# Rotary partner rows by DMA instead of a permutation product, a small chain moved to PSUM, and one activation table for Ln and Exp, in a two-layer hybrid decoder kernel

## The chip, the cores and the metric

The kernel runs on one core of one Trainium2 chip, with five engines that work in parallel and wait for one another by semaphores: TensorE (PE, matrix products; PEld is its weight load), VectorE (DVE), ScalarE (ACT), GpSimd (POOL) and SyncE (SP), which here only issues DMAs. The metric is the device time of one execution in microseconds, lower is better; the time before is the median of three runs.

## The reference, cut to what matters

```python
def reference(x, ln1_g, w_in, qk_norm_g, ...):          # x: 1 x 512 x 1024, two layers
    for l in range(DEPTH):
        h = rmsnorm(x, ln1_g[l])
        proj = h @ w_in[l]                               # 1024 -> 3588 columns
        q = partial_rope(rmsnorm(q, qk_norm_g[l, 0]), cos, sin)   # 4 heads x 2 x 64
        k = partial_rope(rmsnorm(k, qk_norm_g[l, 1]), cos, sin)
        o_a = diff_attention(q, k, v, lam, lambda_init, subln_g[l])
        o_b = sc_b * causal_dwconv(sc_c * sc_h, sc_conv_w[l])
        o_c = s5_mixer(...)                              # diagonal complex scan, 16 groups
        o_d = mamba2_mixer(z, xbc, dt_raw, ...)          # dt = softplus(dt_raw + dt_bias)
        x = x + concat(o_a, o_b, o_c, o_d) @ w_out[l]
        h2 = rmsnorm(x, ln2_g[l])
        g = causal_dwconv(h2 @ ffn_w_gate[l], ffn_conv_w[l])
        x = x + (silu(g) * (h2 @ ffn_w_up[l])) @ ffn_w_down[l]

def partial_rope(x, cos, sin):                           # the first 16 of 64 dimensions
    x1, x2 = x[..., :8], x[..., 8:16]
    rot = concatenate([x1 * cos - x2 * sin, x1 * sin + x2 * cos])
    return concatenate([rot, x[..., 16:]])
```

Dimension i of the first 16 is thus mixed with its partner, dimension i + 8 or i - 8, with a sign. Everything is float32.

## The kernel before

Activations lie transposed, channels on the 128 partitions and the 512 tokens along the row. All products with the large weights go by units: a unit is one block of 128 output channels. Each weight unit passes through four engines. SyncE loads it into one of two `raw` buffers (L260), as soon as GpSimd has read the unit before last (`wl_full`). ScalarE rounds it to a high half `wh` (`prep`, L697). GpSimd computes the low half `wl` = raw - wh (`low`, L287). TensorE then makes three passes over the unit: low activations by `wh` (L386), high by `wh` (L388), high by `wl` (L396), eight products of 128x512 each where the input has 1024 channels. There are two buffers of each kind, so a copy for unit g waits until TensorE has left the high half of unit g - 2. VectorE multiplies the finished bank by the norm factor (`scaled`, L942).

Each engine works through one order written out by hand; a late instruction holds up all behind it. In each layer the 28 units of the input projection come first, numbered s = 0 to 27 below:

- Units 0 and 1 are the S5 input; `dt_rows` and `dt_turn` bring the four step-size columns into bank 5. Units 2 to 7 are the Mamba-2 inputs. VectorE scales each into `pad` and applies four taps (`taps_in_bank`, L959 to L962); ScalarE takes the SiLU from the bank (L790). Between them VectorE computes the step sizes, a softplus by a series, on 128x16 tiles `s16` (`m2_dt`, `m2_log`, `m2_series` with L1021, `m2_steps`). In ScalarE's order, the copy of unit s + 2 comes ahead of the SiLU of unit s and behind that of unit s - 1.
- Units 8 to 15: gate, Mamba-2 products, short convolution. GpSimd makes S5 rotation tables (`table`) and the imaginary part of each S5 scan (`s5_imaginary`) between its low halves.
- Units 16 to 23 are q and k of the four heads, called tiles t = 0 to 7 (t = s - 16); VectorE scales tile t into `G[:, t % 2]`, ScalarE squares it, and after unit 17 + t TensorE makes the group mean (`qk_mean`, L531, bank 4) and the permutation product with the gain folded in (L533, bank 5). ScalarE computes the inverse root by Ln (L715) and Exp (L717); VectorE finishes the tile in `qk_finish`: gain by cosine (L1260), partner by sine (L1262), sum (L1263), norm (L1265, `qk_done`). On every second s VectorE also runs an S5 scan (`s5_scan`), on the others its second half (`s5_back`); before the first tile it waits for the norm of the Mamba-2 output (`m2_rms`).
- Units 24 to 27 are v. Then 16 attention steps (4 heads by 4 query blocks): scores, maxima (L1272), Exp (L832), combination (L1279 to L1281), transpose (L563), product with v (L572); once per head Ln (L842) and Exp (L846) of the output norm. Units of the output projection are put beside some steps (`BESIDE`).

The feed-forward part of a layer is 44 units in and 16 units of 11 blocks down. Which activation table is resident isn't written in the kernel; the build places a load ahead of a function that the resident one doesn't have.

Of the kernel before, what the change touches and what calls it, by code (L numbers as in the profile page):

```python
# [14 lines left out]
L = 2  # L15
# [4 lines left out]
ROPE = 16  # L20
THETA = 500000.0
# [24 lines left out]
for _name, _n in [("ident", P), ("ones", P), ("tri", P), ("perm", P), ("block", P), ("cap", P), ("eps", 1)]:  # L46
    CONSTS[_name] = slice(_o, _o + _n)
    _o += _n
# [3 lines left out]
for _name, _n in [("g1", KD), ("g2", KD), ("qkg", 2), ("subg", 1), ("oneml", 1), ("scw", 6),  # L52
                  ("s5d", 2), ("bglu", 2), ("m2w", 24), ("m2b", 6),
                  ("dtb", M2H), ("alog", M2H), ("m2d", 2), ("m2g", 2), ("ffw", 3 * FF), ("wdt", KD * M2H)]:
    PARAMS[_name] = (_o, _n)
    _o += _n
# [10 lines left out]
def build(nc, A):  # L67
    with ExitStack() as ctx:
# [48 lines left out]
        def early(name, shape, dt=F32):  # L117
# [21 lines left out]
        permg = sb("permg", [P, 2, P])  # L139
# [13 lines left out]
        ident, ones, tri, perm, block1, cap = [  # L153
            cst[:, CONSTS[k]] for k in ("ident", "ones", "tri", "perm", "block", "cap")]
# [38 lines left out]

        sqk_ready, qk_rms, qk_done, v_ready = [sem(n) for n in ("sqk_ready", "qk_rms", "qk_done", "v_ready")]
# [56 lines left out]
        def _(sp):  # L251
# [106 lines left out]
        def _(pe):  # L358
# [167 lines left out]
            def qk_mean(t):  # L526
# [39 lines left out]
            def attend(n):  # L566
                h, q = n // NQ, n % NQ
                if q == 0:
# [15 lines left out]
            for l in range(L):  # L584
# [64 lines left out]
                for n in range(STEPS):  # L649
# [13 lines left out]
                    if n:  # L663
                        attend(n - 1)
                    if n > NQ and n % NQ == 2:
                        head_sum(HEAD_BANK[n // NQ - 1])
                attend(STEPS - 1)
# [15 lines left out]
        def _(act):  # L683
# [34 lines left out]

            def rms():
                act.wait_ge(act_bank[7], nth(act_bank[7]))  # L720
# [27 lines left out]
            for l in range(L):  # L748
# [34 lines left out]
                for s in range(1, NIN):  # L783
# [15 lines left out]
                    if s == 9:  # L799
                        m2_head(0)  # L800
# [50 lines left out]
                for n in range(STEPS):  # L851
# [7 lines left out]
                    if n == 0:  # L859
                        for i, gate in enumerate((sA, sB)):  # L860
                            act.wait_ge(act_bank[i], nth(act_bank[i]))
                            fn(gate[:, :], bank[i][:, :], ACT.Sigmoid, bias=par_of(l, "bglu", i)).then_inc(glu_full, 1)
                    if n == 1:
# [49 lines left out]
        def _(dve):  # L913
# [81 lines left out]

            def m2_dt(l):

                a, e = [s16[:, i, :] for i in (0, 1)]
                by_head = [P, NQ, M2H]
                dve.wait_ge(dve_bank[5], nth(dve_bank[5]))  # L1000
                tt(a.rearrange("p (a b) -> p a b", a=NQ), bank[5][:, 0:16].rearrange("p (a b) -> p a b", a=NQ),
                   par_of(l, "dtb", 0, M2H).unsqueeze(1).broadcast_to(by_head), ADD).then_inc(dve_free[5], 1)
                dve.wait_ge(dve_free[5], freed(dve_free[5]))
                stt(e, a, -1.0, a, MUL, ALU.max).then_inc(dt_abs, 1)
                own(ts(a, a, 0.0, None, ALU.max))

            def m2_log():

                e, s, sq, rec = [s16[:, i, :] for i in (1, 2, 9, 11)]
# [3 lines left out]
                after(tt(s, e, rec, MUL))  # L1013
                own(tt(sq, s, s, MUL))
# [558 lines left out]
```

## Time and profile before

| | |
|---|---|
| median of 3 runs | 1472.79 us (1471.87 to 1472.96) |
| the profiled execution | 1473.24 us, span 1471.4 us |
| TensorE busy | 1395.4 us (95%) |
| VectorE, ScalarE, GpSimd busy | 943.8, 569.9, 685.7 us |
| chain that ended last | 84% TensorE, 10% VectorE, 3% ScalarE |
| input projection of layer one, unit 2 to unit 27 | about 48 to 274 us |
| attention of layer one | about 275 to 366 us |

The profile is one execution on the chip. Its rows give the line of the instruction, the engine, output and inputs by name; an idle time in brackets is followed by what ended it. The "chain that ended last" is followed back from the last instruction, at each step to what released it.

### The profile page before, as it was taken

What the parts mean: (1) busy time and instruction counts of PE and PEld (TensorE: products, weight loads), DVE (VectorE), ACT (ScalarE), POOL (GpSimd) and SP (SyncE); (2) the same over time, 40 slices, a digit from 0 to 9 for tenths busy, and PEclk for the clock granted to TensorE, in tenths of its full rate; (3) what the DMA queues carried; (4) which work ended last, traced back from release to release, by engine and by line L of the source; (5) the groups of instructions that cost most, each with busy time, mean ns of one, the idle gap of its engine ahead of it and who ended that gap; (6) DMA issues with size and microseconds to landing.
All of it is one profiled execution on the core that took longest, in us unless ns stands there. A gap on an engine that the chain in (4) does not pass through costs nothing.

```text
span 1471.4 us, 15836 instructions
## 1 busy us (share of the span) xinstructions
PE 1395.4 (95%) x6116; PEld 1074.4 (73%) x6116; DVE 943.8 (64%) x1221; ACT 569.9 (39%) x805; POOL 685.7 (47%) x368
## 2 busy tenths in 40 slices
PE   3989999798999999999999999998899999999999
PEld 1777656476788888888877775665677888888887
DVE  7778887564677713777228788865657774067740
ACT  3342556456532312222333335645664332123221
POOL 1645768312444443444456456862134444444452
PEclk9999989999999999999999998998999999999999
DMA  5221111111332332323232211111123333223332
GB/s 185 71 73 58 44 53 55 36 33 33 107 101 92 111 98 87 95 91 116 85 100 72 61 55 58 52 42 33 40 54 112 99 100 118 83 86 101 104 101 97
DMA packets 33627, 117.41 MB, mean 80 GB/s; under 512 B 3728, under 2 KB 3856, under 8 KB 33552
## 3 DMA queue, kind: packets, MB, share of 16 engines
q1 hardware_dynamic: 33264, 115.35, 24.9%
q8 instruction: 49, 0.80, 0.2%
q10 hardware_dynamic: 288, 1.05, 0.2%
q14 instruction: 26, 0.21, 0.0%
HBM read 114.28 MB, written 2.10 MB: 79 GB/s over the span
## 4 chain that ended last, share of the span: by engine, by line
PE 84%; DVE 10%; ACT 3%; issue 2%; DMA 1%; POOL 1%; SPq 0%; DVEq 0%; POOLq 0%
PE bank L386 25%; PE bank L388 24%; PE bank L396 24%; PE bank L437 2%; DVE s L1021 1%; PE bank L533 1%; PE bank L448 1%; DVE ml L967 1%; PE bank L446 1%; PE bank L415 1%; PE bank L531 1%; DMA raw<-in_w_first 1%; DVE G L1281 1%; PE bank L572 1%; DVE xl L933 1%
## 5 line engine op out<-in xcount | busy, mean ns | idle before, releaser
L287 POOL TENSOR_TENSOR wl<-raw,wh 128x1024 fp32r<-128x1024 f32 (+3 forms) x208 | 501.7, 2413 | 679.5 <-ACT wh L697 458.5
L386 PE MATMUL bank<-xl,wh 128*128 128x512 f32 x1152 | 303.4, 404 | 35.8 <-ACT wh L697 24.9
L386 PEld LDWEIGHTS bank<-xl,wh 128*128 128x128 f32 x1152 | 217.8, 192 | 109.7 <-issue 39.7
L697 ACT ACTIVATE wh<-raw 128x1024 fp32r<-128x1024 f32 (+3 forms) x208 | 218.3, 1050 | 196.9 <-PE bank L388 191.2
L388 PE MATMUL bank<-xh,wh 128*128 128x512 f32 x1152 | 287.9, 392 | 0.0
L396 PE MATMUL bank<-xh,wl 128*128 128x512 f32 x1152 | 286.1, 390 | 0.0
L388 PEld LDWEIGHTS bank<-xh,wh 128*128 128x128 f32 x1152 | 218.5, 190 | 46.1
L396 PEld LDWEIGHTS bank<-xh,wl 128*128 128x128 f32 x1152 | 216.4, 188 | 45.2 <-issue 0.3
L971 DVE TENSOR_TENSOR x<-x,bank 128x512 f32<-128x512 f32 x64 | 44.0, 687 | 219.7 <-PE bank L396 219.7
L386 PE MATMUL bank<-ml,wh 128*128 128x512 f32 x512 | 136.3, 408 | 0.0
L388 PE MATMUL bank<-mh,wh 128*128 128x512 f32 x512 | 128.4, 391 | 0.0
L396 PE MATMUL bank<-mh,wl 128*128 128x512 f32 x512 | 127.5, 389 | 0.0
L386 PEld LDWEIGHTS bank<-ml,wh 128*128 128x128 f32 x512 | 97.8, 194 | 24.5 <-issue 3.0
L388 PEld LDWEIGHTS bank<-mh,wh 128*128 128x128 f32 x512 | 96.9, 189 | 20.9
L396 PEld LDWEIGHTS bank<-mh,wl 128*128 128x128 f32 x512 | 96.1, 188 | 20.0
L1303 DVE TENSOR_TENSOR G<-G 128x512 f32<-128x512 f32 x44 | 105.2, 2391 | 4.6
L893 ACT ACTIVATE G<-G 128x512 f32<-128x512 f32 x44 | 27.8, 632 | 204.4 <-DVE G L954 204.4
L949 DVE TENSOR_SCALAR G<-pad,par_all 128x512 f32<-128x512 f32 x48 | 94.3, 1964 | 1.5
L942 DVE TENSOR_TENSOR G<-bank,rbc 128x512 f32<-128x512 f32 x76 | 52.2, 687 | 63.7 <-PE bank L396 61.4
L942 DVE TENSOR_TENSOR pad<-bank,rbc 128x512 f32<-128x512 f32 x60 | 41.4, 691 | 53.9 <-PE bank L396 43.3
L896 ACT ACTIVATE mh<-G 128x512 fp32r<-128x512 f32 x44 | 27.7, 630 | 111.1 <-DVE G L1303 111.1
L1305 DVE TENSOR_TENSOR ml<-G,mh 128x512 fp32r<-128x512 f32 x44 | 47.3, 1074 | 31.2 <-ACT mh L896 31.2
(264 smaller groups left out, 1529.9 us busy)
## 6 DMA issues: line engine op xcount, KB each, us to landing
raw<-in_w_gu SPq DMA_DIRECT2D x88, 512.0 KB, 3.5
raw<-in_w_in SPq DMA_DIRECT2D x52, 512.0 KB, 3.5
raw<-in_w_dn SPq DMA_DIRECT2D x32, 704.0 KB, 4.1
raw<-in_w_oe SPq DMA_DIRECT2D x16, 384.0 KB, 3.0
raw<-in_w_ol SPq DMA_DIRECT2D x16, 256.0 KB, 2.6
x<-in_x SPq DMA_DIRECT2D x8, 256.0 KB, 6.1
raw<-in_w_first SPq DMA_DIRECT2D x4, 512.0 KB, 6.7
out_x<-x SPq DMA_DIRECT2D x8, 256.0 KB, 4.7
```

The costliest lines, as they stand in the source:

```text
L287: tt(wl[:, p, 0:cols], raw[:, p, 0:cols], wh[:, p, 0:cols].bitcast(F32), ALU.subtract).then_inc(wl_full, 1)
L386: mm(bank[b][:, :], wh[:, p, k * P:(k + 1) * P], lo[:, k, :], start=(k == 0), stop=False)
L388: w = mm(bank[b][:, :], wh[:, p, k * P:(k + 1) * P], hi[:, k, :], start=False, stop=False)
L396: w = mm(bank[b][:, :], wl[:, p, k * P:(k + 1) * P], hi[:, k, :], start=False, stop=(k == K - 1))
L437: mm(bank[2 + c][:, :], bmat[r:r + SH, c, j // 4, :], u[r:r + SH, j // 4, :], start=True, stop=True).then_inc(dve_bank[2 + c], 1)
L697: fn(wh[:, p, 0:cols], raw[:, p, 0:cols], ACT.Copy).then_inc(wh_full, 1)
L893: fn(G[:, 1, :], G[:, 0, :], ACT.Silu).then_inc(g_silu, 1)
L942: tt(out, bank[b][:, :], rbc[:, :], MUL).then_inc(unit_out, 1)
L949: after(ts(out, pad[:, p, 4:4 + T], weights[n - 1], None, MUL))
L971: tt(x[:, o, :], x[:, o, :], bank[p][:, :], ADD).then_inc(resid, 1)
L1303: tt(G[:, 3, :], G[:, 1, :], G[:, 2, :], MUL).then_inc(h_ready, 1)
L1305: tt(ml[:, i, :], G[:, 3, :], mh[:, i, :].bitcast(F32), SUB).then_inc(hid_ready, 1)
```

## The change

1. *Partner rows.* The host permutes the columns of q and k so that the rotated dimensions of both components of a head lie in partitions 48 to 79, with partners in neighbouring rows. SyncE, ahead of the weight load of unit s + 4, waits until VectorE has written q/k unit s, and issues two DMAs of 16 rows each, which copy even rows onto odd ones and back into a `partner` buffer (one is `G[:, 5]`, one is new). `qk_finish` multiplies this buffer by a gain of its own (`partg`) and by the sines, which VectorE has copied once per layer into bank 5, and writes into bank 4. The permutation product, its matrix and its scaled copies go. The mean product now claims bank 4 against `qk_done`. Before the first tile of a layer VectorE clears both buffers.
2. *Step sizes.* Intermediate results of the softplus chain (`raw_dt`, `rec`, `q`) move from `s16` to columns of bank 5; `m2_dt` writes its sum twice, to `s16` and to the bank, and `m2_log` the quotient twice, so the chain has 20 instructions in place of 18.
3. *ScalarE's order.* The SiLU of unit s comes one step later, so the copy of unit s + 3 is now ahead of it. The Exp of the decays goes a step later as well.
4. *Tables.* The set that holds both Ln and Exp is loaded explicitly before the norms, after each gelu and sigmoid, and before the Mamba-2 exponentials.

```diff
@@ SyncE's loop over the weight units
                 if g >= 2:
                     sp.wait_ge(wl_full, g - 1)
+                s = g % (len(UNITS) // L) - 4
+                if 16 <= s < 24:
+                    sp.wait_ge(unit_out, unit_out_of(g // (len(UNITS) // L), s))
+                    for to, of in ((0, 1), (1, 0)):
+                        sp.dma_start(partner[s % 2][ROT0 + to:ROT1:2, :],
+                                     G[ROT0 + of:ROT1:2, s % 2, :]).then_inc(partner_in[s % 2], 16)
                 sp.dma_start(raw[:, g % 2, 0:cols], src[l, i]).then_inc(raw_full[g % 2], 16)
@@ TensorE, qk_mean
-                claim(4, act_free[4])
+                claim(4, qk_done)
                 mm(bank[4][:, :], block1, G[:, 2, :], start=True, stop=True).then_inc(act_bank[4], 1)
-                claim(5, qk_done)
-                mm(bank[5][:, :], permg[:, t % 2, :], G[:, t % 2, :], start=True, stop=True).then_inc(dve_bank[5], 1)
@@ TensorE, attend
+                if n == 0:
+                    pe.wait_ge(qk_done, 8 * (l + 1))
@@ ScalarE
+            def ln_exp_tables():
+                nc.scalar.preload_act_table_set("natural_log_exp_and_others")
             def rms():
+                ln_exp_tables()
                 act.wait_ge(act_bank[7], nth(act_bank[7]))
...
-                    if 2 <= s <= 7:
+                    if 3 <= s <= 8:
                         act.wait_ge(conv_out, nth(conv_out))
-                        fn(xbc[:, s - 2, :], bank[unit_bank(s)][:, :], ACT.Silu).then_inc(xbc_silu, 1)
-                    if s == 6:
+                        fn(xbc[:, s - 3, :], bank[unit_bank(s - 1)][:, :], ACT.Silu).then_inc(xbc_silu, 1)
+                    if s == 7:
                         act.wait_ge(decay_go, nth(decay_go))
...
                     if s == 9:
+                        ln_exp_tables()
                         m2_head(0)
@@ VectorE, parameters
+                ts(par_of(l, "partg"), par_of(l, "partg"), QK ** -0.5, None, MUL)
-                for i in range(2):
-                    ts(permg[:, i, :], perm, par_of(l, "qkg", i), None, MUL)
@@ VectorE, step sizes
+            def small(i):
+                return bank[5][:, 32 + 16 * i:48 + 16 * i]
...
-                e, s, sq, rec = [s16[:, i, :] for i in (1, 2, 9, 11)]
+                e, s, sq, rec = s16[:, 1, :], s16[:, 2, :], s16[:, 9, :], small(1)
                 after(ts(rec, e, 2.0, None, ADD))
                 after(nc.vector.reciprocal(rec, rec))
-                after(tt(s, e, rec, MUL))
-                own(tt(sq, s, s, MUL))
+                tt(s, e, rec, MUL)
+                after(tt(rec, e, rec, MUL))
+                own(tt(sq, rec, s, MUL))
...
-                sq, q = [s16[:, i, :] for i in (9, 10)]
+                sq, q = s16[:, 9, :], small(2)
                 after(ts(q, sq, 1.0 / 17, None, MUL))
                 for c in (15, 13, 11, 9, 7, 5, 3):
                     after(stt(q, q, 1.0 / c, sq, ADD, MUL))
@@ VectorE, qk_finish
-                dve.wait_ge(dve_bank[5], nth(dve_bank[5]))
-                after(tt(bank[5][:, :], bank[5][:, :], sinT, MUL))
-                after(tt(bank[5][:, :], q, bank[5][:, :], ADD))
+                dve.wait_ge(partner_in[p], 32 * (4 * l + t // 2 + 1))
+                dve.wait_ge(act_free[4], nth(act_free[4]))
+                after(stt(bank[4][:, :], partner[p], par_of(l, "partg", p), bank[5][:, :], MUL, MUL))
+                after(tt(bank[4][:, :], q, bank[4][:, :], ADD))
                 dve.wait_ge(qk_rms, nth(qk_rms))
-                tt(q, bank[5][:, :], G[:, 3 + p, :], MUL).then_inc(qk_done, 1)
+                tt(q, bank[4][:, :], G[:, 3 + p, :], MUL).then_inc(qk_done, 1)
@@ VectorE, step s == 15
                         s5_back(l, 1)
+                        nc.vector.memset(partner[0], 0.0)
+                        nc.vector.memset(partner[1], 0.0)
+                        dve.wait_ge(yz_ready, 2 * (l + 1))
+                        own(copy(bank[5][:, :], sinT))
```

## Rows read from the trace of the kernel before

**Rows 1.** The page: busy time of the engines; the chain that ended last.

```profile
PE 1395.4 (95%) x6116; PEld 1074.4 (73%) x6116; DVE 943.8 (64%) x1221; ACT 569.9 (39%) x805; POOL 685.7 (47%) x368
...
PE 84%; DVE 10%; ACT 3%; issue 2%; DMA 1%; POOL 1%; SPq 0%; DVEq 0%; POOLq 0%
```

**Rows 2.** TensorE's waits: line, releaser, us in total, times, longest.

```profile
PE bank L386 <- ACT wh L697: 24.9, 5, 17.5
```

**Rows 3.** Windows: two rotary units; after an attention wait.

```profile
core 0: us, PE busy (x) PEld busy (x) DVE busy (x) ACT busy (x) POOL busy (x), PEclk, DMA share, GB/s
207.93:226.45 18.52, 18.52 (x65) 11.38 (x65) 15.30 (x22) 12.57 (x16) 15.58 (x12) 1.00 0.17 57
...
347.70:352.00 4.30, 4.30 (x11) 2.69 (x10) 1.46 (x3) 4.24 (x7) 0.00 (x0) 0.50 0.02 4
```

**Rows 4.** TensorE's timeline, convolution stage, both layers: start, us, [idle before <- releaser].

```profile
80.61 3.78 PE L386 MATMUL bank<-xl,wh 128*128 128x512 f32 x8 [4.20 <-ACT wh L697]
...
799.05 3.66 PE L386 MATMUL bank<-xl,wh 128*128 128x512 f32 x8 [2.66 <-ACT wh L697]
```

**Rows 5.** Timelines of VectorE, GpSimd and ScalarE, first layer, convolution stage.

```profile
68.02 7.74 DVE L1021 SCALAR_TENSOR_TENSOR s<-s 128x16 f32<-128x16 f32 x7
...
75.80 1.27 POOL L311 TENSOR_TENSOR ex<-ex,s5h 128x512 f32<-128x512 f32 x1
...
79.01 0.60 ACT L790 ACTIVATE xbc<-bank 128x512 f32<-128x512 f32 x1 [11.37 <-DVE bank L962]
```

**Rows 6.** Two lines of VectorE alone: count, then ns as min/median/max.

```profile
L1021 DVE SCALAR_TENSOR_TENSOR s<-s x14: 174/973/2424, 68.0 to 793.2; 128x16 f32<-128x16 f32 x14
...
L961 DVE SCALAR_TENSOR_TENSOR bank<-pad,par_all,bank x24: 754/756/757, 56.9 to 809.2; 128x512 f32<-128x512 f32 x24
```

**Rows 7.** Timelines of TensorE and ScalarE in attention, first layer.

```profile
324.96 0.44 PE L563 MATMUL bank<-cst,G 128*128 128x128 f32 x2 [1.59 <-DVE G L1281]
...
331.98 1.28 ACT L842 ACT_TABLE_LOAD   x1
...
343.06 0.44 PE L563 MATMUL bank<-cst,G 128*128 128x128 f32 x2 [1.61 <-DVE G L1281]
344.59 0.49 PE L572 MATMUL bank<-G,v 128*128 128x128 f32 x2 [1.09 <-DVE ssum L1288]
346.16 0.90 PE L563 MATMUL bank<-cst,G 128*128 128x128 f32 x3 [1.09 <-DVE G L1281]
```

**Rows 8.** The chain that ended last, convolution stage: start, us, what.

```profile
56.46 1.81 PE bank L388 x8
...
84.39 2.58 PE bank L388 x8
```

**Rows 9.** The same chain in the rotary stage of the first layer.

```profile
185.42 2.08 PE bank L533 x2
...
199.57 0.86 PE bank L533 x2
```

**Rows 10.** Timelines of GpSimd and VectorE in the rotary stage, around tile 3.

```profile
206.29 2.39 POOL L287 TENSOR_TENSOR wl<-raw,wh 128x1024 fp32r<-128x1024 f32 x1
...
207.97 0.69 DVE L942 TENSOR_TENSOR G<-bank,rbc 128x512 f32<-128x512 f32 x1 [2.39 <-PE bank L396]
...
210.15 0.69 DVE L1262 TENSOR_TENSOR bank<-bank,rotary 128x512 f32<-128x512 f32 x1
```

**Rows 11.** DMA issues by line: KB each, median us from issue to landing.

```profile
raw<-in_w_ol SPq DMA_DIRECT2D x16, 256.0 KB, 2.6
...
wglu<-in_wglu SPq DMA_DIRECT2D x2, 256.0 KB, 7.3
```

**Rows 12.** The issues of SyncE at the start.

```profile
2.11 4.39 SPq L256 DMA_DIRECT2D x<-in_x  x8
```

**Rows 13.** VectorE's memset of a 128x512 tile: ns as min/median/max.

```profile
L975 DVE MEMSET ssum<- x3: 485/485/485, 367.7 to 1085.1; 128x512 f32 x3
```

**Rows 14.** VectorE's timeline ahead of the first rotary tile.

```profile
166.59 2.59 DVE L1390 SCALAR_TENSOR_TENSOR xbc<-xbc,par_all,z 128x512 f32<-128x512 f32 x2 [2.60 <-ACT z L717]
```

More of the change, by code:

```diff
@@ L45 @@
 CONSTS, _o = {}, 0
-for _name, _n in [("ident", P), ("ones", P), ("tri", P), ("perm", P), ("block", P), ("cap", P), ("eps", 1)]:
+for _name, _n in [("ident", P), ("ones", P), ("tri", P), ("block", P), ("cap", P), ("eps", 1)]:
     CONSTS[_name] = slice(_o, _o + _n)
@@ L138, in build @@
         rho_all = sb("rho_all", [P, L, SJ])
-        permg = sb("permg", [P, 2, P])
+        partner1 = sb("partner", [P, T])
+        partner = (G[:, 5, :], partner1[:, :])
         par_all = sb("par_all", [P, L, NPAR])
@@ L151, in build @@
         bank = [ctx.enter_context(nc.psum_tensor(f"bank{b}", [P, T], F32)) for b in range(8)]
-        ident, ones, tri, perm, block1, cap = [
-            cst[:, CONSTS[k]] for k in ("ident", "ones", "tri", "perm", "block", "cap")]
+        ident, ones, tri, block1, cap = [
+            cst[:, CONSTS[k]] for k in ("ident", "ones", "tri", "block", "cap")]
         cosT, sinT = rotary[:, 0, :], rotary[:, 1, :]
@@ L192, in build @@
         em_full, em_high, mixed_ready = sem("em_full"), sem("em_high"), sem("mixed_ready")
+        partner_in = [sem(f"partner_in{p}") for p in range(2)]
         sqk_ready, qk_rms, qk_done, v_ready = [sem(n) for n in ("sqk_ready", "qk_rms", "qk_done", "v_ready")]
@@ L564, in turn, with attend @@
                 w.then_inc(act_bank[4], 1)
-            def attend(n):
+            def attend(l, n):
                 h, q = n // NQ, n % NQ
+                if n == 0:
+                    pe.wait_ge(qk_done, 8 * (l + 1))
                 if q == 0:
@@ L663, in _ @@
                     if n:
-                        attend(n - 1)
+                        attend(l, n - 1)
                     if n > NQ and n % NQ == 2:
                         head_sum(HEAD_BANK[n // NQ - 1])
-                attend(STEPS - 1)
+                attend(l, STEPS - 1)
                 unit(0, KEARLY, early_hi, early_lo, resid)
@@ L994, in dt_scaled @@
                 freed(dve_free[5])
+            def small(i):
+                return bank[5][:, 32 + 16 * i:48 + 16 * i]
             def m2_dt(l):
-                a, e = [s16[:, i, :] for i in (0, 1)]
+                a, e, raw_dt = s16[:, 0, :], s16[:, 1, :], small(0)
                 by_head = [P, NQ, M2H]
                 dve.wait_ge(dve_bank[5], nth(dve_bank[5]))
[L1001 to L1005, printed above, removed]
+                for out in (a, raw_dt):
+                    w = tt(out.rearrange("p (a b) -> p a b", a=NQ), bank[5][:, 0:16].rearrange("p (a b) -> p a b", a=NQ),
+                           par_of(l, "dtb", 0, M2H).unsqueeze(1).broadcast_to(by_head), ADD)
+                after(w)
+                stt(e, raw_dt, -1.0, a, MUL, ALU.max).then_inc(dt_abs, 1)
+                dve.wait_ge(dt_abs, l + 1)
+                own(ts(a, raw_dt, 0.0, None, ALU.max))
             def m2_log():
-                e, s, sq, rec = [s16[:, i, :] for i in (1, 2, 9, 11)]
+                e, s, sq, rec = s16[:, 1, :], s16[:, 2, :], s16[:, 9, :], small(1)
                 dve.wait_ge(dt_exp, nth(dt_exp))
@@ L1023, in m2_steps @@
             def m2_steps():
-                a, s, q = [s16[:, i, :] for i in (0, 2, 10)]
+                a, s, q = s16[:, 0, :], s16[:, 2, :], small(2)
                 by_head = [P, NQ, M2H]
@@ L1028, in m2_steps @@
                 after(stt(q, q, 1.0, s, ADD, MUL))
[L1029 removed]
+                stt(a, q, 2.0, a, MUL, ADD).then_inc(dve_free[5], 1)
+                dve.wait_ge(dve_free[5], freed(dve_free[5]))
                 stt(adt.rearrange("p (a b) -> p a b", a=NQ), a.rearrange("p (a b) -> p a b", a=NQ), -1.0,
@@ L1448, in _ @@
                         residual(o, o % 2)
+PAIRS = [d for i in range(ROPE // 2) for d in (i, i + ROPE // 2)]
+PLAIN = list(range(ROPE, QK))
+QK_ROWS = [(0, d) for d in PLAIN + PAIRS] + [(1, d) for d in PAIRS + PLAIN]
 def constants():
@@ L1461, in constants @@
     half = ROPE // 2
-    for b in range(2):
-        for i in range(half):
-            lo, hi = b * QK + i, b * QK + half + i
-            perm[hi, lo], perm[lo, hi] = -1, 1
-            cos[lo], cos[hi] = np.cos(ang[:, i]), np.cos(ang[:, i])
-            sin[lo], sin[hi] = np.sin(ang[:, i]), np.sin(ang[:, i])
-    c[:, CONSTS["perm"]] = perm
+    for row, (_, dim) in enumerate(QK_ROWS):
+        if dim < ROPE:
+            cos[row] = np.cos(ang[:, dim % half])
+            sin[row] = np.sin(ang[:, dim % half]) * (-1 if dim < half else 1)
     c[:, CONSTS["block"]] = r[:, None] // QK == r[None, :] // QK
@@ L1488, in layout @@
     for h in range(HEADS):
-        order += [w[:, :, h * P:(h + 1) * P], w[:, :, a + h * P:a + (h + 1) * P]]
+        rows = np.array([h * P + c * QK + d for c, d in QK_ROWS])
+        order += [w[:, :, rows], w[:, :, a + rows]]
     w_in = units(np.concatenate(order + [w[:, :, b:c]], axis=2))
@@ L1508, in layout @@
     put("g2", tiled(inp["ln2_g"]))
-    put("qkg", np.tile(inp["qk_norm_g"], (1, 1, 2)).transpose(0, 2, 1))
+    dims = np.array([d for _, d in QK_ROWS])
+    put("qkg", inp["qk_norm_g"][:, :, dims].transpose(0, 2, 1))
+    partner = np.where(dims < ROPE, (dims + ROPE // 2) % ROPE, dims)
+    put("partg", inp["qk_norm_g"][:, :, partner].transpose(0, 2, 1))
     put("subg", tiled(inp["subln_g"]))
```

8 lines of the change are left out of this document (5 added, 3 removed).

## The prediction

> **What bounds the kernel now.** Read the page first. TensorE is busy for 95% of the span and the chain that ended last is 84% TensorE [rows 1], so time can come from two places only: products that leave TensorE, and stretches in which it stands still. The largest of its waits is 24.9 us for the high weight halves; 17.5 us of that is the first weights at the start, which nothing here touches [rows 2]. A stall costs more than its length: in the stretch after one of them (347.7 us) the granted clock is 0.50, the level of 1.2 GHz, against 1.00 in the rotary stage, where TensorE never rests [rows 3]. So each stall is priced with the slow products behind it.
>
> *Convolution stage (units 2 to 7).* TensorE waits 4.20 us in the first layer and 2.66 us in the second for unit 7's high halves, and its first products after that are at half speed [rows 4]. Who is late? VectorE's seven L1021 instructions, 128x16 each, take 7.74 us while GpSimd computes; then come the taps of unit 4; only after them can ScalarE take the SiLU (79.01) [rows 5], and the weight copy of unit 7 stands behind that SiLU in ScalarE's order. An L1021 takes 174 ns undisturbed and up to 2424; L961, whose output and one input lie in PSUM, takes 754 to 757 ns in all 24 cases, in the same stretch [rows 6]. I read this as all-SBUF VectorE work standing behind GpSimd, and PSUM work not.
>
> *Rotary stage.* Two units take 18.52 us, all of it TensorE's; VectorE is busy for 15.30 of it and GpSimd for 15.58 [rows 3]. *Attention.* ScalarE loads a table before each Ln and another before the next Exp; TensorE waits 1.59 us the first time, then 1.61, 1.09 and 1.09 us [rows 7].
>
> **The change, part by part.** Sums are against the profiled execution: 1473.24 us, span 1471.4; it lies 0.45 us above the median.
>
> *Step-size chain in PSUM, SiLUs one step later.* The 18 small instructions become 20. The price of a small one in PSUM is not in the trace: below, 0.17 us as undisturbed in SBUF; above, the 1.1 us of now. I take 0.2 us with the gap between two, because L961 shows no disturbance. The seven L1021 then take 1.4 instead of 7.74 us. VectorE has 1.6 us of series and some 3.8 us of scaling and taps (five instructions of about 0.76) for a unit of 3 x 1.81 = 5.4 us: it just keeps up. Besides, unit 7's copy now stands behind the SiLU of unit 3, which is long done. GpSimd is next in line: its table ends at 77.07 [rows 5], the low half of unit 7 takes 2.4 us more, to 79.5; TensorE wants it two passes after 76.4, at 80.0. The margin is 0.5 us, so a new stall is priced at nothing here, and in R3 below if the cover is gone. Gain, first layer: 4.20 + (3.78 - 1.81) + (2.58 - 1.81) = 6.9 us; second: 2.66 + (3.66 - 1.81) = 4.5 [rows 4, 8]. Together **11.4 us**.
>
> The SBUF page of the Trainium skill ("Who interferes with whom") says that a VectorE instruction with two SBUF inputs contends with a GpSimd instruction that reads SBUF. By it every moved step with one PSUM input escapes, the same sum as from L961; L1260, both inputs in SBUF, goes on paying.
>
> *No permutation product.* Each cost 0.86 us, and once per layer 2.08 us at half clock behind a wait [rows 9]. Eight go per layer. The first is no gain, since VectorE sets the pace there. Nor is the second: the product that stays now itself waits for the previous tile (bank 4 is claimed against qk_done), starts where the removed one did and takes its 2.08 us. The other six save 6 x 0.86 = 5.2 us a layer, **10.3 us** in all, if VectorE and GpSimd can follow at 18.52 - 1.72 = 16.8 us for two units.
>
> Can they? GpSimd needs 15.58: yes, 1.2 us over. VectorE needs 15.30, plus 2 x 0.07 for scalar_tensor_tensors in place of tensor_tensors (L961 against 0.69), plus waits. One is for ScalarE's Ln, which comes behind the scan copies and a weight copy on every second tile; I estimate 1 us. The other is new: the partner rows. SyncE issues them only when GpSimd has ended the low half two units on; for tile 3 that is at 206.29 + 2.39 = 208.7, and VectorE wants the rows at 210.15 [rows 10]. A transfer of 2.6 us [rows 11] behind one other issue of 0.55 us (8 in 4.39 us [rows 12]) lands at 211.8: 1.7 us late on odd tiles, hardly on even ones. 15.4 + 1.0 + 1.7 = 18.1 would be over 16.8, but VectorE reaches the pair 2.39 us before TensorE has it [rows 10], and TensorE wants the result only a unit later; I charge 1 us a layer: **-2.0 us**. The trace has no small SBUF transfer. Below, its price is near nothing; above, the 7.3 us of wglu at the crowded start [rows 11]; I take 2.6, the smallest of the same queue in steady state. The weight load behind it on SyncE is delayed by two issues, and its copy comes some 10 us later. SyncE's wait on VectorE's output of four units ago is always over; GpSimd's order is unchanged.
>
> The DMA page of the Trainium skill ("Anatomy of one DMA") gives about 2.0 us fixed cost; by that 32 KB would land 0.5 us sooner than I say, and the charge would halve. No row of this trace shows it.
>
> *Before the first tile.* VectorE gets two memsets (485 ns, the same in all three of the old ones [rows 13]) and a copy into bank 5 (0.69, as L942), 1.65 us in all. They fall into its 2.60 us wait for m2_rms [rows 14], which itself ends 1.28 us earlier without the table load between Ln and Exp. So the first tile comes about 1 us earlier, and with it the product waiting at 185.4: **+2.0 us** for both layers. Were the memsets to stand behind GpSimd, this would be a loss of 1 us a layer.
>
> *Common table.* In attention two loads of 1.283 us drop out between probabilities and next scores, 2.56 us each time. The first time the wait of 1.59 us goes entirely; the second time the chain to the product at 346.16 comes 2.56 us earlier, against 3.8 us of waiting [rows 7]. (1.59 + 2.56) x 2 = **8.3 us**. After that wait 4.3 us ran at clock 0.50 [rows 3], about 2 us lost a layer. Of the wait 1.2 us stays; whether the clock still falls I can't read off, so I take half of 4: **+2.0**. Loads elsewhere hide behind TensorE's work: the norm's Ln and Exp run beside the 5.4 us of unit 1.
>
> *Small.* 64 KB of constants less ahead of the first weights, of some 3.5 MB in 16 us: **0.3 us**. In the parameters two 128-column instructions go and one of 2 columns comes, behind the down products. The added wait in attend repeats one that TensorE has made before the scores: nothing.
>
> **Sum:** 11.4 + 10.3 - 2.0 + 2.0 + 8.3 + 2.0 + 0.3 = 32.3. 1473.24 - 32.3 = 1440.9; less 0.45, about **1440.5 us**.
>
> **Rivals.** *R1: the rotary stage stays bound, by VectorE or GpSimd.* For it: 15.4 and 15.6 of 16.8 us, and late partners. The stage then gives 8.3 less: 1449. Against: the lead above. 18%.
> *R2: the table loads stay*: the build places one before each Ln and Exp as now, or the explicit ones come on top. For it: the loads are there although one set would do. 8.3 + 2.0 + 1 go: 1452. 8%.
> *R3: the convolution stall moves to GpSimd*, by the margin of 0.5 us, or to the decay Exp, now a step later and behind another weight copy. Half of 11.4 goes: 1446. 10%.
> *R4: slower.* One mechanism: the partner rows land after 7.3 us like wglu. Each of 12 tiles holds VectorE up 4.7 us beyond the 2.6, and through qk_done the next product: 12 x 4.7 = 56, less 32.3: 1496. It decides from a landing of 2.6 + 32.3 / 12 = 5.3 us on. Against: there megabytes are in flight, here the queue is empty. 4%.
>
> **Numbers.** The sum 60%, R1 18, R3 10, R2 8, R4 4. The likeliest case's own range is 1435 to 1446: clock term at 0 or 4, transfers free or at 4 us. For 8 in 10, R1, R3 and the edge of R2 come in: 1434 to 1452. About 0.2% (3 us) is what a measurement can tell from no change. Faster 0.94, same 0.02, slower 0.04.
>
> **What would show it.** After: L1021 near 0.18 us each, no TensorE wait for wh but the first, clock 1.00 around 80 us; two rotary units in 16.8 us (R1: 17.5 to 18.5, TensorE waiting for s5e or qk); VectorE waiting for the partner on odd tiles; no table loads at Ln and Exp; the attention waits of 1.6 us gone. Wrong if PSUM operands don't spare the small instructions, if weights come late behind SyncE's new waits, or if the memsets stand behind GpSimd.

## The result, and the profile after

The changed kernel takes **1432.34 us** (median of 4 runs, 1431.66 to 1433.96) beside 1472.74 for the kernel before: ratio 0.9728, 95% interval 0.9712 to 0.9745, 40.4 us gained. Forecast were 1440.5 us and a range of 1434 to 1452: faster as said, but by 8 us more than the sum, and 1.7 us outside the range. The profiled execution took 1431.66 us, span 1429.8.

The page of the changed kernel, its busy times and its chain:

```profile
PE 1366.9 (96%) x6084; PEld 1060.8 (74%) x6084; DVE 925.3 (65%) x1229; ACT 500.7 (35%) x751; POOL 686.7 (48%) x368
...
PE 81%; DVE 11%; POOL 2%; issue 2%; ACT 2%; DMA 1%; SPq 1%; DVEq 0%; POOLq 0%
```

TensorE lost 28.5 us of busy time against [rows 1], more than the 13.8 us of the 16 products removed (0.86 each); the rest are products that ran at half speed before. ScalarE lost 69 us: it makes 30 table loads in place of 84, at 1.283 us each.

TensorE's waits in the changed kernel:

```profile
PE bank L395 <- ACT wh L706: 19.0, 3, 17.5
...
PE bank L540 <- DVE qk L1290: 4.8, 2, 2.4
PE bank L570 <- DVE G L1306: 4.2, 5, 1.2
...
PE bank L446 <- DVE s5e L1184: 3.0, 5, 0.7
```

Its small step-size instructions (L1044, count, then ns as min/median/max):

```profile
L1044 DVE SCALAR_TENSOR_TENSOR bank<-bank,s x14: 182/182/183, 66.7 to 765.0; 128x16 f32<-128x16 f32 x14
```

Against [rows 2] the wait for wh has lost the convolution stalls, and TensorE stands still nowhere between 70 and 90 us, at a granted clock of 1.00. The seven small instructions of [rows 6] take 182 ns each instead of up to 2424, though GpSimd is busy beside them as before (5.92 of the 6 us from 66 us on). The partner rows of odd tiles, by issues, waits and landings (nobody waits for those of even tiles):

```profile
L267 SPq DMA_DIRECT2D partner<-G x16: 507/548/953, 175.6 to 931.3; - x16
...
  DVE bank L1287: 8.3, 6
...
DMA to landing us min/median/max: 1.7/1.8/2.5
```

The transfer lands 1.8 us after its issue, less than the 2.6 taken. VectorE waits for it in 6 of the 8 odd tiles, 1.4 us each; 1.7 was forecast. TensorE's timeline at the place in attention where [rows 7] have the wait of 1.59 us (L563, now L570):

```profile
307.85 0.39 PE L570 MATMUL bank<-cst,G 128*128 128x128 f32 x2
308.00 1.17 PE L395 MATMUL bank<-ml,wh 128*128 128x512 f32 x4
```

The transposes start with no wait before them.

Where along the span did the lead arise? Each unit of the input projection is scaled once by VectorE (L942, now L959), as soon as TensorE has it. The difference between the start of the same scaling in two traces is the lead of one kernel over the other at that unit; what is added between two units belongs to the stage between them. In us, for each layer (first + second):

| stage | forecast | whole change | tables alone | chain alone | tables in attention alone | all but the rotary part |
|---|---|---|---|---|---|---|
| start, up to unit 2 | 0.3 | -0.3 | -0.5 | 0.3 | 0.2 | 0.0 |
| unit 2 to 8 (convolution) | 6.9 + 4.5 | 6.9 + 4.5 | 4.0 + 0.0 | 6.9 + 4.5 | 0.0 + 1.0 | 6.9 + 4.5 |
| unit 8 to 18 (up to tile 2) | 1.0 + 1.0 | 3.2 + 3.2 | 2.9 + 2.9 | 0.0 + 0.0 | 0.0 + 0.1 | 2.9 + 2.8 |
| unit 18 to 27 (later tiles, v) | 4.15 + 4.15 | 3.9 + 3.5 | 2.1 + 1.7 | 0.1, -0.5 | 0.0, -0.9 | 0.5 + 0.1 |
| unit 27 to the feed-forward part | 5.15 + 5.15 | 8.9 + 7.7 | 7.0 + 9.2 | 0.0 + 2.4 | 7.5 + 9.4 | 7.0 + 7.8 |
| sum | 32.3 | 41.6 | 29.2 | 13.9 | 17.2 | 32.5 |

The last four columns are experiments 2, 3, 4 and 1 below. All are single executions, and single executions scatter. The 1.0 and -0.9 of the tables in attention are of this kind. So are some 2 us in the last row of the second layer: from 997 to 1005 us the trace of the kernel before has a granted clock of 0.57, that of the ScalarE order alone (experiment 3) has 1.00 there and gains 2.0 us in this row, and by its runs that kernel gains nothing. The columns therefore sum to more than the runs give (41.6 to 40.1, 29.2 to 25.8, 13.9 to 10.8, 17.2 to 14.6 us). Already the third column says where to look: the convolution term is exact, the late tiles nearly, and the surplus lies at the first tiles and in attention, both places with table loads.

### The profile page after: what moved, and what is told of

Same layout as the page of the kernel before. It is cut to its first block, busy times and chain, and to the rows that moved or that the text cites. A ratio compares the mean times of both kernels' runs of the same rounds, so it can differ in the third digit from the quotient of the medians.

```text
span 1429.8 us, 15792 instructions
## 1 busy us (share of the span) xinstructions
PE 1366.9 (96%) x6084; PEld 1060.8 (74%) x6084; DVE 925.3 (65%) x1229; ACT 500.7 (35%) x751; POOL 686.7 (48%) x368
## 4 chain that ended last, share of the span: by engine, by line
PE 81%; DVE 11%; POOL 2%; issue 2%; ACT 2%; DMA 1%; SPq 1%; DVEq 0%; POOLq 0%
PE bank L395 24%; PE bank L397 24%; PE bank L405 24%; PE bank L446 2%; PE bank L581 1%; DVE bank L1166 1%; DVE bank L1168 1%; PE bank L424 1%; PE bank L560 1%; DMA raw<-in_w_first 1%; DVE xl L950 1%; PE bank L570 1%; POOL wl L296 1%; PE bank L457 1%; POOL s5im L329 1%
## 5 line engine op out<-in xcount | busy, mean ns | idle before, releaser
L395 PE MATMUL bank<-xl,wh 128*128 128x512 f32 x1152 | 300.2, 402 | 29.3 <-ACT wh L706 19.0
L1328 DVE TENSOR_TENSOR G<-G 128x512 f32<-128x512 f32 x44 | 108.6, 2469 | 5.3 <-DVE G L959 0.9
L959 DVE TENSOR_TENSOR G<-bank,rbc 128x512 f32<-128x512 f32 x76 | 52.2, 687 | 59.3 <-PE bank L405 57.0
L959 DVE TENSOR_TENSOR pad<-bank,rbc 128x512 f32<-128x512 f32 x60 | 41.5, 691 | 56.8 <-PE bank L405 48.6
```

The costliest lines, as they stand in the source:

```text
L395: mm(bank[b][:, :], wh[:, p, k * P:(k + 1) * P], lo[:, k, :], start=(k == 0), stop=False)
L959: tt(out, bank[b][:, :], rbc[:, :], MUL).then_inc(unit_out, 1)
L1328: tt(G[:, 3, :], G[:, 1, :], G[:, 2, :], MUL).then_inc(h_ready, 1)
```

## The experiments

Gains are worked out from the ratio to the runs of the kernel before on the same chip, times 1472.7 us.

**1. All but the rotary part.** The changed kernel with

```diff
-                claim(4, qk_done)
+                claim(4, act_free[4])
                 mm(bank[4][:, :], block1, G[:, 2, :], start=True, stop=True).then_inc(act_bank[4], 1)
+                claim(5, qk_done)
+                mm(bank[5][:, :], permg[:, t % 2, :], G[:, t % 2, :], start=True, stop=True).then_inc(dve_bank[5], 1)
```

and `qk_finish`, the memsets, SyncE's transfers and the constants as before.

> The changed kernel with its rotary part undone: permutation product, sines in SBUF, no partner DMAs, no memsets; the PSUM chain, the SiLU order and the common tables stay. Theory A (terms as forecast: six products per layer less VectorE's lateness, 8.3, plus 0.7 of the first tile that memset placement can touch): 1432.3 + 8 to 9 = 1440.5 to 1441.5 us. Theory B (the surplus of about 3.6 us in the two rotary stages belongs to the rotary part too, because it leaves TensorE's first product and VectorE's alignment to GpSimd better): 1444 to 1446 us. Theory C (the rotary stage was bound by VectorE, the product cost nothing): within 3 us of 1432.3.

1439.69 us, ratio 0.9777 (0.976 to 0.9793): 7.2 us more than the changed kernel. That is nearest to Theory A, a little less: six products less the lateness are the size that was said, and the rotary part is not where the surplus comes from.

**2. The common table alone.** The kernel before with

```diff
+            def ln_exp_tables():
+                nc.scalar.preload_act_table_set("natural_log_exp_and_others")
```

called in `rms`, after gelu, at s = 9 and after the sigmoids.

> The kernel before with the explicit loads of one common table alone. Theory A (as forecast: 8.3 us of loads in attention, 2.0 of slow clock, up to 1.28 a layer ahead of the first tile): 1472.7 - 10.3 to 12.9 = 1460 to 1462.5 us, and the 1.6 us waits of TensorE in attention are gone. Theory B (the whole surplus in attention, 8.9 and 7.7 us gained by TensorE where 5.2 a layer was forecast, belongs to the tables): 1472.7 - 16.6 to 19 = 1454 to 1456 us. Theory C (the surplus comes from a new alignment of VectorE to GpSimd that only the whole change gives): as A, and VectorE's combination in front of the first transpose still takes 2.08 us.

1445.47 us, ratio 0.9825 (0.9803 to 0.9847): **25.8 us** from the tables alone, two and a half times what was forecast and more than either theory gave. All three theories fall, C also because the combination takes 0.48 us here and not 2.08. Of the 29.2 us of the profiled execution 16.2 lie in attention, 9.6 at the tiles, where the forecast had 2.0, and 4.0 in the first convolution stage. ScalarE did this before, at tiles 0 and 1 of the first layer (timeline):

```profile
177.66 1.28 ACT L715 ACT_TABLE_LOAD   x1
178.95 0.69 ACT L715 ACTIVATE G<-bank,cst 128x512 f32<-128x512 f32 x1
179.66 1.28 ACT L717 ACT_TABLE_LOAD   x1
180.95 0.63 ACT L717 ACTIVATE G<-G 128x512 f32<-128x512 f32 x1
181.49 0.61 ACT L764 ACTIVATE G<-G 128x512 f32<-128x512 f32 x1
```

TensorE at the same place:

```profile
182.16 1.13 PE L531 MATMUL bank<-G,cst 128*128 128x512 f32 x2 [1.46 <-ACT G L764]
185.42 2.08 PE L533 MATMUL bank<-G,permg 128*128 128x512 f32 x2 [2.14 <-DVE qk L1265]
187.43 3.78 PE L437 MATMUL bank<-u,bmat 32*128 32x512 f32 x4
191.14 3.78 PE L386 MATMUL bank<-xl,wh 128*128 128x512 f32 x8
```

With the common table ScalarE does the same without a load:

```profile
172.81 0.68 ACT L715 ACTIVATE G<-bank,cst 128x512 f32<-128x512 f32 x1
173.52 0.63 ACT L717 ACTIVATE G<-G 128x512 f32<-128x512 f32 x1
174.05 0.62 ACT L769 ACTIVATE G<-G 128x512 f32<-128x512 f32 x1
```

and TensorE:

```profile
177.05 1.02 PE L531 MATMUL bank<-G,cst 128*128 128x512 f32 x2
179.07 1.12 PE L533 MATMUL bank<-G,permg 128*128 128x512 f32 x2 [1.00 <-DVE qk L1273]
180.99 2.10 PE L437 MATMUL bank<-u,bmat 32*128 32x512 f32 x4 [0.80 <-DVE s5e L1168]
183.02 3.54 PE L386 MATMUL bank<-xl,wh 128*128 128x512 f32 x8
```

ScalarE squares tile 1 (L764, L769) behind the Ln and Exp of tile 0. With two loads in front it ended at 182.1, and TensorE waited 1.46 us for it, then 2.14 more for VectorE, before the product of [rows 9]; without them the mean product runs unhindered and the two waits left are 1.00 and 0.80. The four products for S5, 3.78 us at a granted clock of 0.50 (1.2 GHz), run in 2.10; the eight behind them are still slow (3.54 us, clock 0.55). Two loads of 1.28 us were on the path here.

**3. The chain alone, and the ScalarE order alone.** The kernel before with the step-size functions of the changed one; and the kernel before with

```diff
-                    if 2 <= s <= 7:
+                    if 3 <= s <= 8:
                         act.wait_ge(conv_out, nth(conv_out))
-                        fn(xbc[:, s - 2, :], bank[unit_bank(s)][:, :], ACT.Silu).then_inc(xbc_silu, 1)
-                    if s == 6:
+                        fn(xbc[:, s - 3, :], bank[unit_bank(s - 1)][:, :], ACT.Silu).then_inc(xbc_silu, 1)
+                    if s == 7:
```

> The kernel before with the step-size chain in PSUM alone; the order of the SiLUs stays. Theory A (VectorE's slow small instructions are the cause of the convolution stall): 1472.7 - 11.4 = 1461.3 us, no TensorE wait for wh but the first, clock 1.00 behind it. Rival (ScalarE's order is needed as well, since the copy of unit 7 stands behind the SiLU of unit 4): a rest of the stall of 1 to 3 us per layer with its slow clock stays, 1464 to 1468 us.

> The kernel before with the SiLUs (and the decay Exp) one step later in ScalarE's order alone; the chain stays in SBUF. Theory A (the slow chain is the cause): the stall moves to the next copy or to a bank that waits for its SiLU, 1466 to 1472 us. Rival (the order is the cause: VectorE's lateness would be absorbed if no weight copy stood behind it): the stall goes entirely though the small instructions stay at about 1.1 us, 1461 to 1463 us.

The chain alone: 1461.46 us, 0.9927 (0.9912 to 0.9942), 10.8 us gained, 6.93 and 4.55 of it in the convolution stage by the table above. The order alone: 1472.92 us, 1.0005 (0.9996 to 1.0014), nothing. TensorE in the convolution stage with the order alone:

```profile
84.71 0.81 PE L470 MATMUL bank<-cst,xbc 128*128 128x128 f32 x4 [1.93 <-ACT xbc L790]
87.99 1.11 PE L470 MATMUL bank<-cst,xbc 128*128 128x128 f32 x4 [2.47 <-DVE s L1168]
88.76 3.54 PE L386 MATMUL bank<-xl,wh 128*128 128x512 f32 x8
```

The stall for the weight copy is gone and stands a unit later, at the transposes (L470), 1.93 us for a SiLU and 2.47 for VectorE, with the slow clock behind it (0.51 from 88.8 to 92 us). So VectorE's slow chain is the cause, and the order in ScalarE only chooses who meets it first.

The trace of the tables alone adds to this. In its first layer the seven small instructions, still in SBUF, take 5.21 us:

```profile
66.94 5.21 DVE L1029 SCALAR_TENSOR_TENSOR s<-s 128x16 f32<-128x16 f32 x7
```

They started while GpSimd stood still for 0.92 us (66.6 to 67.5), and TensorE's stall at unit 7 is gone: these are the 4.0 us of that column. In its second layer they take 7.84 us as before, and the stall of 2.66 us is there. With the chain in PSUM the 4.0 us can't be gained twice: chain and tables give 10.8 and 25.8 us alone, and 32.8 together (experiment 1).

**4. The common table in attention alone.** The kernel before, with the load placed only behind the second gelu and behind the sigmoids.

> The kernel before with the common table loaded only after the second gelu and after the sigmoids, so that the table loads go from the attention steps and stay in the input projection. With all common loads the trace gained 7.0 and 9.2 us behind the last scaled unit of the projection, and 3.5 + 5.0 + 4.5 us before it. Theory A (the two parts are worth what the ledger says): 1472.7 - 16 = 1456 to 1458 us. Theory B (my forecast for attention, 8.3 to 10.3, was right, and the rest of the gain there was handed on from the projection): 1462 to 1464 us. Theory C (the tables count only in the projection): above 1466 us.

1457.82 us, 0.9901 (0.9887 to 0.9914): 14.6 us, and by the trace 7.5 and 9.4 in the attention of the two layers (2.1 of the 9.4 are the scatter at 997 to 1005 us), nothing systematic elsewhere. Theory A. TensorE at the fourth head with this kernel:

```profile
339.43 0.39 PE L563 MATMUL bank<-cst,G 128*128 128x128 f32 x2
339.66 0.39 PE L572 MATMUL bank<-G,v 128*128 128x128 f32 x2
341.28 0.55 PE L563 MATMUL bank<-cst,G 128*128 128x128 f32 x3 [1.24 <-DVE G L1287]
...
342.57 1.96 PE L386 MATMUL bank<-ml,wh 128*128 128x512 f32 x6
344.37 1.53 PE L388 MATMUL bank<-mh,wh 128*128 128x512 f32 x6
```

In the kernel before [rows 7] the same three products waited 1.61, 1.09 and 1.09 us; now only the third waits, 1.24. With the 1.59 us of the third head, 5.38 us of waits have become 1.24: 4.14 are gone. The unit behind them takes 1.80 us to its second pass instead of 3.34:

```profile
348.64 3.55 PE L386 MATMUL bank<-ml,wh 128*128 128x512 f32 x6
351.98 1.60 PE L388 MATMUL bank<-mh,wh 128*128 128x512 f32 x6
```

The lead grows from 3.63 us at the first of the three (343.06 - 339.43) to 4.88 at the third and to 7.61 at 351.98. Of the 7.61, 0.1 was there before attention, 4.14 are the waits, 0.65 are products that ran longer beside a wait, and 2.7 came behind the third product, where the clock of the kernel before fell to 0.50 and here stays at 1.00. One thing more went with the loads. VectorE's combination ahead of the transpose at 324.96 [rows 7], in the kernel before:

```profile
322.82 2.08 DVE L1281 SCALAR_TENSOR_TENSOR G<-G,soft 128x256 f32<-128x256 f32 x1
```

GpSimd in the kernel before:

```profile
322.82 1.80 POOL L287 TENSOR_TENSOR wl<-raw,wh 128x768 fp32r<-128x768 f32 x1 [7.06 <-ACT wh L697]
```

and VectorE with the tables of attention alone, where GpSimd's low half begins at 322.26:

```profile
320.56 0.48 DVE L1287 SCALAR_TENSOR_TENSOR G<-G,soft 128x256 f32<-128x256 f32 x1
```

Both tensor inputs are in SBUF. Made late by the loads, the instruction started in the same moment as GpSimd's low half and took 2.08 us instead of 0.48; the same pair stands at the fourth head (340.92). The Trainium skill's page "SBUF — State Buffer" ("Who interferes with whom") says that such an instruction contends with a GpSimd instruction that reads SBUF; the rows agree. The loads thus made VectorE late by 2 x 1.28 us and by 1.6 more through the collision. TensorE got only part of this back. The first wait could give no more than its 1.59 us. At the fourth head the Exp behind the combination now stands behind a weight copy (337.63 to 338.47), and the chain to the third product comes 3.0 us earlier, of which 2.55 show as waits that are gone.

**5. Partner rows from ScalarE's queue.** In the changed kernel SyncE's two issues go, and ScalarE makes them ahead of its square:

```diff
                     act.wait_ge(unit_out, unit_out_of(l, 16 + t))
+                    for to, of in ((0, 1), (1, 0)):
+                        act.dma_start(partner[t % 2][ROT0 + to:ROT1:2, :],
+                                      G[ROT0 + of:ROT1:2, t % 2, :]).then_inc(partner_in[t % 2], 16)
```

> The changed kernel with the two partner DMAs issued by ScalarE right after its wait for the scaled tile, ahead of the square, instead of by SyncE two units later. The rows then land some 3 us after the tile is scaled; VectorE waits 8.3 us for them now. Theory A (their lateness is a term of the sum, forecast at -2.0 us): VectorE waits for no partner, 1429.5 to 1431 us. Theory B (the lateness lies beside other waits and costs nothing): 1431.5 to 1433 us. Rival on the other side (the issues take ScalarE's time ahead of the square, 1 us a tile, and delay the mean): 1434 to 1440 us.

1428.40 us, 0.9703 (0.969 to 0.9716), 3.7 us better than the changed kernel; by the leads in the later tiles 2.6. VectorE waits for no partner. Theory A: the lateness was a real term. That it was larger than the 2.0 charged is not shown, since the two intervals leave about 3 us of doubt. The issues take ScalarE about 1.2 us a tile, and no delay shows from them.

**6. Another bank for odd tiles.** `b = (4, 7)[t % 2]` for the mean product, its Ln and `qk_finish`.

> The changed kernel with the group means of odd tiles in bank 7 instead of bank 4, so that the mean product no longer waits for the tile before to be finished. Theory A (TensorE's wait of 2.4 us at tile 1 only moves to the next product, which waits for VectorE's s5e at about the same time): 1430 to 1432.5 us, 0 to 2 us gained, the wait stands at the product of u by bmat. Theory B (the wait itself is the cost, with the slow clock behind it, 2.4 + 4.8 us a layer): 1418 to 1425 us.

1431.29 us, 0.9722 (0.9709 to 0.9735): about 1 us, less than the two intervals can tell from nothing: Theory A. The wait moved, as TensorE's timeline of this kernel shows:

```profile
172.13 1.02 PE L543 MATMUL bank<-G,cst 128*128 128x512 f32 x2
176.53 2.86 PE L446 MATMUL bank<-u,bmat 32*128 32x512 f32 x4 [3.38 <-DVE s5e L1188]
179.32 3.78 PE L395 MATMUL bank<-xl,wh 128*128 128x512 f32 x8
```

**7. The low halves of the Mamba-2 output later.** The changed kernel with

```diff
-                    if s == 17:
-                        for i in range(2):
-                            emit_low(MIXD + i, xbc[:, 4 + i, :])
...
                         (s5_back if s % 2 else s5_scan)(l, (s - 12) // 2)
+                    if s == 18:
+                        for i in range(2):
+                            emit_low(MIXD + i, xbc[:, 4 + i, :])
```

> The changed kernel with VectorE's two subtractions for the low halves of the Mamba-2 output (1.79 us each, behind a wait of 1.5 us for ScalarE's copy) moved from before tile 0 is finished to the end of the step after. Theory A (what makes TensorE wait 2.4 us for tile 0, and run slow behind it, is VectorE's order ahead of tile 0, not the table or the partner): the wait and the slow clock at about 176 us go, 2.4 + 4.8 us a layer less what comes back in later tiles, 1418 to 1426 us. Theory B (VectorE is the bound of the whole stage, so a moved instruction changes nothing): 1431 to 1433 us. Rival on the other side: over 1434 us.

1424.57 us, 0.9676 (0.9663 to 0.969), 7.7 us better than the changed kernel. TensorE in the changed kernel:

```profile
175.65 2.05 PE L540 MATMUL bank<-G,cst 128*128 128x512 f32 x2 [2.42 <-DVE qk L1290]
177.62 3.78 PE L446 MATMUL bank<-u,bmat 32*128 32x512 f32 x4
181.33 3.78 PE L395 MATMUL bank<-xl,wh 128*128 128x512 f32 x8
```

and with the low halves later:

```profile
173.56 1.06 PE L540 MATMUL bank<-G,cst 128*128 128x512 f32 x2
175.35 1.98 PE L446 MATMUL bank<-u,bmat 32*128 32x512 f32 x4 [0.74 <-DVE s5e L1184]
177.26 2.09 PE L395 MATMUL bank<-xl,wh 128*128 128x512 f32 x8
```

The mean product of tile 1 no longer waits 2.42 us, and what follows runs at a granted clock of 1.00 (2.4 GHz) instead of 0.50. What VectorE had ahead of tile 0 was a wait of 1.55 us and the two subtractions, 2.40 us together; the 1.79 us of the expectation is another instruction (L1284). It is VectorE's order ahead of tile 0 that held TensorE. By the leads of the first layer it gains 2.6 us up to tile 2 and 2.6 more up to tile 4, and gives 2.2 back by unit 26, where other waits are next.

**8. The changed kernel without the common table.**

> The changed kernel without the explicit loads of the common table; the PSUM chain, the SiLU order and the rotary part stay. The tables alone took 26.5 us from the kernel before, the chain alone 11, the rotary part 7.4 on top of both. Theory A (the table loads delayed the same tiles and stalls as the rest, so parts overlap little): 1472.6 - 11 - 7.4 = 1454 us, up to 1458. Theory B (without the common table the late Ln and Exp bind the tiles, and the rotary part gives nothing): 1461 to 1463 us.

1459.98 us, 0.9923 (0.991 to 0.9937): 11.3 us below the kernel before, as much as the chain alone (0.9927). That lies between the theories and nearer B: with the loads in place the rotary part gives nothing that can be told. TensorE at tile 1 of this kernel:

```profile
178.50 2.05 PE L540 MATMUL bank<-G,cst 128*128 128x512 f32 x2 [5.68 <-DVE qk L1290]
180.48 3.77 PE L446 MATMUL bank<-u,bmat 32*128 32x512 f32 x4
```

and one of VectorE's waits:

```profile
DVE bank L1287 <- ACT G L724: 12.1, 8, 2.5
```

TensorE waits 5.68 us there, and VectorE 12.1 us in 8 times for ScalarE's Ln. The product saved is waited away.

**9. Products put back.** In the changed kernel, from tile 2 on, one more product of the same size into bank 7, which nobody reads:

```diff
+                if t >= 2:
+                    pe.wait_ge(*free_at[7])
+                    mm(bank[7][:, :], block1, G[:, t % 2, :], start=True, stop=True)
```

> The changed kernel with one more group-mean product per tile from tile 2 on, into bank 7, which nobody reads: 12 products of 0.86 us put back on TensorE, all else as changed. Theory A (TensorE sets the pace of the rotary stage now, with VectorE's lateness beside it): + 10.3 us, 1442 to 1443 us. Theory B (VectorE's order sets the pace, as its rival said): less than half of that, 1432 to 1437 us, and TensorE's waits for VectorE in the stage (3.0 us in 5) vanish.

1440.07 us, 0.9782 (0.9769 to 0.9795): 8.0 us more. Between the theories and nearer A: of 12 x 0.86 = 10.3 us three quarters are TensorE's own time. Its waits for s5e fell from 3.0 us to 0.7, which is the 2.3 us missing.

**10. What gained, together.** The low halves later and the partner rows from ScalarE; then the second bank as well.

> Both single steps that gained, together: the Mamba-2 low halves after tile 1 (8 us alone), and the partner DMAs issued by ScalarE (4 us alone). With the low halves moved VectorE waits 14.0 us for partners, more than the 8.3 of the changed kernel. Theory A (the two add up or more): 1419 to 1421 us, VectorE waits for no partner. Theory B (both take from the same slack of VectorE): 1423 to 1425 us.

> The one before with the means of odd tiles in bank 7 too. Alone that gained about 1 us and moved the wait. Theory A (TensorE is ahead of VectorE at the first tile only, and the rest of that wait moves again): as the kernel before in this list within 1 us. Theory B (with VectorE earlier the bank claim is what is left of the waits, 1.5 us and the slow clock behind it): 2 to 4 us less than it.

**1415.70 us**, 0.9619 (0.9605 to 0.9632), and 1414.67 us, 0.9614 (0.9601 to 0.9627): 16.1 and 16.8 us better than the changed kernel. The two steps give more together than alone (7.7 + 3.7): with the low halves later alone, VectorE waited 14.0 us for the partners of odd tiles and 3.9 for those of even ones, and with both steps for none; the second bank gives nothing that can be told. Windows over the same 32 us of the changed kernel and of the first of these:

```profile
core 0: us, PE busy (x) PEld busy (x) DVE busy (x) ACT busy (x) POOL busy (x), PEclk, DMA share, GB/s
165.00:197.00 32.00, 29.58 (x90) 17.48 (x89) 26.10 (x33) 12.84 (x19) 24.89 (x17) 0.84 0.19 56
```

and

```profile
165.00:197.00 32.00, 31.45 (x115) 20.25 (x113) 29.91 (x43) 14.76 (x22) 30.75 (x22) 1.00 0.24 75
```

TensorE's granted clock goes from 0.84 to 1.00 and its idle time from 2.4 to 0.6 us.

## Why the prediction was right in most of its parts and short in its sum

- **Convolution stage, 11.4 us: right.** 6.93 + 4.55 by the trace, 10.8 by the runs of the chain alone. The small instructions take 0.18 us, seven of them 1.48 with their gaps where 1.4 was taken. The reading of [rows 6], that an operand in PSUM spares them, held. The sum gave all to the chain and nothing to the SiLU order, and the order alone gave nothing.
- **Six products a layer less lateness, 10.3 - 2.0: right.** 7.2 us by the runs of experiment 1; 8.0 of the 10.3 came back in experiment 9; the lateness cost 2.6 us by the leads and 3.7 by the runs where 2.0 were charged. The term stands only on the common table, which the prediction did not see: it priced the two parts as independent.
- **The common table: the step that failed.** On top of the chain it gave 22.0 us by the runs (32.8 in experiment 1 less 10.8) where 2.0 + 8.3 + 2.0 = 12.3 were forecast. Two terms were too small, in two places.
- **Before the first tile, +2.0: 6.2 us in experiment 1** (2.86 + 2.82 and 0.47 + 0.05 in the table of stages; the chain alone gave nothing in these stages). The step that failed is the sentence "Loads elsewhere hide behind TensorE's work". It was checked for the norm of unit 1 and taken over for the tiles. In them two loads stood ahead of the squares, and at tile 1 TensorE waited for that square, 1.46 us at 182.16, a row above the one that I quoted in [rows 9]. Behind this wait and the next its products ran at clock 0.50. The memsets lay where they were put, in the wait for m2_rms, and cost nothing that shows: in the trace after they take 0.48 us each beside a busy GpSimd, and VectorE finds m2_rms there when they end.
- **Attention, 8.3 + 2.0: 14.6 us by the runs, 16.9 by the trace.** The wait terms were right: "(1.59 + 2.56) x 2 = 8.3" is 4.15 a layer, and 4.14 are gone in the first. This is partly luck. The chain at the fourth head came 3.0 us earlier and not 2.56, since the collision with GpSimd went too and a weight copy came in between. The step that failed is "I take half of 4: +2.0", 1.0 a layer. In the first layer 2.7 us of slow clock went behind the third wait, and 0.65 more on products beside the waits. The bound of 4 for both layers was itself too low: it priced only the 4.3 us at clock 0.50, and between 343 and 347.7 us the clock was down as well (0.74).
- **Start, +0.3: not seen.** -0.3 in this execution; the thirteen traces of changed kernels, laid against the kernel before, lie between -0.8 and +0.9 there.
- **The rivals.** R2 (the loads stay) is out: the loads at Ln and Exp are gone. R3 is out, since the chain alone gives the whole convolution term. R1 is partly true: TensorE waits 3.0 us for s5e in the later tiles, but two units take 16.84 us in the best pair and 17.48 in another, against 16.8 forecast. R4 is out at a landing of 1.8 us; a landing of 5.3 would have decided it. The Trainium skill's page "DMA: Bandwidth & Descriptors" ("Anatomy of one DMA") has about 2.0 us of fixed cost, but fitted on transfers that GpSimd issues. These are issued by SyncE, so their 1.8 us lies near that figure and doesn't test it. Nor would that figure have halved the charge, as the prediction has it: rows that land 0.5 us sooner are 1.2 us late instead of 1.7.
- **The range.** The likeliest case was 1435 to 1446 by its own bounds, and the lower end of 1434 came from it. Its two terms at their best, 2 us each, make 1436.5 and not 1435. It lacked the bound that mattered: loads at other places were set to 0 with no upper end. A load is 1.283 us, and a layer has 8 tiles with two of them; by my estimate a quarter of that on the path (10.3 us) would have opened the range to about 1430.

**Left open.** Which of the loads in the input projection cost what at the tiles was not tried one by one: the tables of the projection were only taken out together. How the 9.4 us of the second attention divide into waits and clock was not worked out beyond the scatter named above.

## What to carry to other kernels

Activation table loads are priced by where they stand, not by how many there are: follow each one to the next instruction of ScalarE that another engine waits for, and ask at every such row what is late without it. A part priced alone can be worth nothing until another part is made; here the removed product paid only with the common table. When an engine's clock falls behind a wait, look for the instruction that can be moved from before the wait to after it: two subtractions moved by one step gave 7.7 us, about as much as removing twelve products.

## What the runs showed that was not expected

- A transfer of 32 KB within SBUF, one of two issued back to back, lands 1.7 to 2.5 us after its issue, and its issue takes SyncE 0.55 us. From ScalarE's queue, in the first kernel of experiment 10, it is 1.8 to 4.0 us, 2.5 in the median, and still early enough.
- An explicit load of the table that holds Ln and Exp keeps the build from placing its own: 1.28 us twice per tile go (84 loads become 30), and the Exp starts 0.72 us after the start of the Ln.
- A wait of 2.42 us at tile 1 cost TensorE 4.5 us more in slow products: (2.05 - 1.06) + (3.78 - 1.98) + (3.78 - 2.09), by the rows of experiment 7; the granted clock of the changed kernel is 0.70 over the 17 us from 172 us on, and 1.00 with the low halves later, where a wait of 0.74 us is left.
